# Packed products with their passes grouped by the weight's part, another order of the opening, and the memory heads' turns one product sooner

## The reference

```python
h = rms_norm(x, g_pre)                                    # 512 x 2048
proj = h @ w_in          # qa ka va ga | qb kb vb gb | fb | qm gm : widths 4*768, 4*768, 6, 2*512
out_a = moba_attention(qa, ka, va, rel_bias)              # 6 heads of 128, T5 bias
out_b = forgetting_attention(qb, kb, vb, cumsum(log_sigmoid(fb + b_forget)))   # 6 heads
km, vm = split(rms_norm(mem, g_mem) @ w_mem_kv)           # memory: 256 x 2048 -> 2 * 512
out_m = memory_attention(qm, km, vm)                      # 4 heads, 256 memory tokens
y = concat([out_a * silu(ga), out_b * silu(gb), out_m * silu(gm)])
out = x + rms_norm(y @ w_out, g_post)
```

## Time and profile before

| | us |
|---|---|
| median of 3 runs | 901.62 (901.34 to 902.13) |
| profiled execution | 902.28 |
| its span, first to last instruction | 900.5 |
| TensorE busy | 871.3 |
| VectorE busy | 733.1 |
| ScalarE busy | 537.8 |
| strips of the memory and opening, until the first packed pass | 186.8 |
| one pair of packed strips | 45.0 |

### The profile page before, as it was taken

One profiled execution on the slowest core, in us unless ns is written; L12 is line 12 of the kernel. 1 busy time (PEld: TensorE's weight loads), 2 busy tenths in 40 slices (PEclk: granted clock), 3 DMA queues, 4 the chain that ended last, 5 costly groups with the idle time before them and its releaser, 6 DMA issues.

```text
span 900.5 us, 13815 instructions
## 1 busy us (share of the span) xinstructions
PE 871.3 (97%) x5181; PEld 764.1 (85%) x5181; DVE 733.1 (81%) x1070; ACT 537.8 (60%) x932; POOL 76.6 (9%) x84
## 2 busy tenths in 40 slices
PE   8998999999999999999999999999999999999995
PEld 6888998987888888888888888888888877778884
DVE  5889978888888888888888888888988885975558
ACT  5794665555656565656565656565656585565452
POOL 0000220000000000000030303030301000000000
PEclk9999999999999999999999999999999999999998
DMA  9961567467668568667667667567653397465854
GB/s 304 284 167 48 164 165 154 118 174 164 165 142 210 151 167 185 154 175 177 152 176 175 153 175 175 152 176 175 152 129 106 130 364 272 154 220 189 290 199 186
DMA packets 179143, 161.37 MB, mean 179 GB/s; under 512 B 7353, under 2 KB 144217, under 8 KB 177670
## 3 DMA queue, kind: packets, MB, share of 16 engines
q1 hardware_dynamic: 169942, 141.62, 51.2%
q0 software_dynamic: 8704, 16.78, 13.6%
q10 hardware_dynamic: 432, 2.10, 0.7%
HBM read 152.33 MB, written 43.28 MB: 217 GB/s over the span
## 4 chain that ended last, share of the span: by engine, by line
PE 71%; DVE 15%; ACT 8%; issue 5%; POOL 1%; DVEq 0%; ACTq 0%; POOLq 0%
PE d_ps L703 18%; PE e_ps L703 10%; PE d_ps L705 9%; PE e_ps L705 5%; PE c_ps L703 4%; DVE ring L1459 3%; PE pt_ps L810 3%; ACT ring L1017 3%; PE c_ps L705 2%; PE d_ps L653 2%; PE d_ps L655 2%; PE d_ps L654 2%; DVE sums L1486 2%; PE score_ps L654 1%; PE score_ps L655 1%
## 5 line engine op out<-in xcount | busy, mean ns | idle before, releaser
L1459 DVE TENSOR_TENSOR ring<-raw,ring 128x1024 fp32r<-128x1024 f32 x134 | 164.7, 1231 | 53.1 <-ACT ring L1017 53.0
L703 PE MATMUL d_ps<-late,ring 128*128 128x512 f32 x576 | 206.6, 398 | 1.2 <-DVE five L1586 1.2
L1459 DVE TENSOR_TENSOR ring<-sums,ring 128x1024 fp32r<-128x1024 f32 x112 | 137.6, 1228 | 52.2 <-ACT ring L1017 51.9
L1017 ACT ACTIVATE ring<-raw 128x1024 fp32r<-128x1024 f32 x134 | 140.6, 1058 | 43.8 <-PE d_ps L655 17.2
L705 PE MATMUL d_ps<-late,ring 128*128 128x256 f32 x576 | 161.5, 280 | 0.0
L703 PEld LDWEIGHTS d_ps<-late,ring 128*128 128x128 f32 x576 | 108.1, 188 | 26.4 <-DVE five L1586 1.5
L1017 ACT ACTIVATE ring<-sums 128x1024 fp32r<-128x1024 f32 x112 | 118.1, 1055 | 20.0 <-DVE sums L1486 18.4
L705 PEld LDWEIGHTS d_ps<-late,ring 128*128 128x128 f32 x576 | 108.8, 189 | 0.0
L703 PE MATMUL c_ps<-tok,ring 128*128 128x512 f32 x192 | 69.3, 400 | 0.0
L703 PE MATMUL e_ps<-late,ring 128*128 128x512 f32 x192 | 69.1, 399 | 0.0
L703 PE MATMUL e_ps<-tok,ring 128*128 128x512 f32 x192 | 69.0, 399 | 0.0
(11 more groups left out here) (392 smaller groups left out, 2001.5 us busy)
## 6 DMA issues: line engine op xcount, KB each, us to landing
raw<-in_w_in_dram SPq DMA_DIRECT2D x112, 512.0 KB, 5.4
sum_dram<-in_w_out_dram POOLq DMA_DIRECT2D x32, 512.0 KB, 7.4
raw<-sum_dram SPq DMA_DIRECT2D x32, 512.0 KB, 3.9
raw<-in_w_out_dram SPq DMA_DIRECT2D x24, 512.0 KB, 7.3
raw<-in_w_mem_kv_dram SPq DMA_DIRECT2D x16, 512.0 KB, 8.6
sum_dram<-in_w_out_dram SPq DMA_DIRECT2D x16, 512.0 KB, 6.4
sum_dram<-sum_dram SPq DMA_DIRECT2D x16, 512.0 KB, 6.0
stage<-in_x_dram SPq DMA_DIRECT2D x4, 1024.0 KB, 9.7
```

The source lines that it names most:

```text
L703: pe.matmul(bank[:], w[:, 0, k], both[:, k], start=i in (TOK_A, TOK_B) and k == 0, stop=False, skip_group_check=True)
L1017: act.activation(dst, src, ACTF.Copy).then_inc(hi_done, 1)
L1459: return dve.tensor_tensor(dst, a_, hi_.bitcast(F32), ALU.subtract)
```

## The change

1. In a packed product the 8 passes with the high weight part come first, after a wait for the high part alone, then the 8 with the low part.
2. The opening: the gains are loaded on ScalarE's queue and the memory tiles on SyncE's; of 14 warm-up products 4 stay and 10 go between the two halves of the first turn; ScalarE and VectorE take memory banks and weight pieces in another order; the statistics of the memory come in t = 1 and its spread in t = 2; the squares of a token tile come one t later; the key strips are taken in t = 2, 3, 3 and 4 (`KEYS_DURING`), strips 0, 1 and 2 keeping three banks; the value strips' splits and turns and the first operands move among each other.
3. A memory head's turn comes after product D (i = 3) and its product with the values after F (i = 5), with the splits in step.

```diff
-SQUARE_DURING = {0: 2, 1: 3, 2: 4, 3: 5}
-SCALE_DURING = {1: 2, 2: 3, 3: 4, 4: 5}
+SQUARE_DURING = LOAD_DURING
+SCALE_DURING = LOAD_DURING
+KEYS_DURING = {2: (0,), 3: (1, 2), 4: (3,)}
...
-KEEP_WARM = 14
+KEEP_WARM = 4
+BETWEEN_HALVES = 10
...
+        def mem_strip(t):
+
+            bank = (d_ps + [e_ps])[t] if t < 3 else d_ps[(t - 3) % 2]
+            return bank[:, 0:NMEM]
...
-                if t >= 2:
-                    pe.wait_ge(mem_free, t - 1)
+                if t >= 3:
+                    pe.wait_ge(mem_free, t - 2 if t < 5 else t - 1)
...
-                pe.wait_ge(lo_done, operand(p, i) + 1)
...
+                if packed(p):
+                    pe.wait_ge(hi_done, operand(p, i) + 1)
+                    for k in range(KH):
+                        pe.matmul(bank[:], w[:, 0, k], both[:, k], start=i in (TOK_A, TOK_B) and k == 0, stop=False,
+                                  skip_group_check=True)
+                pe.wait_ge(lo_done, operand(p, i) + 1)
                 for k in range(KH):
                     if packed(p):
-                        pe.matmul(bank[:], w[:, 0, k], both[:, k], start=i in (TOK_A, TOK_B) and k == 0, stop=False,
-                                  skip_group_check=True)
                         last = pe.matmul(bank[:, T2:S], w[:, 1, k], hi[:, k], start=False, stop=k == KH - 1,
                                          skip_group_check=True)
...
-                if t == 1:
+                if t == 2:
                     spread_rstd()
...
             forget_gates(1, TOK_D, slice(0, T2))
-            turn_v_mem(NM - 1)
             pe.wait_ge(bank_taken, TURNS)
             forget_gates(3, TOK_F, slice(T2, S))
+            turn_v_mem(NM - 1)
...
-                    if i == 4:
+                    if i == 3:
                         turn_probs(head, 0)
                         turn_probs(head, 1)
-                    if i == 6:
+                    if i == 5:
                         prob_times_v(head)
...
+                if t in SQUARE_DURING:
+                    squares(SQUARE_DURING[t])
+                    root(SQUARE_DURING[t], SQUARE_DURING[t])
+                for m in KEYS_DURING.get(t, ()):
+                    act.wait_ge(mem_free, m + 1)
+                    act.activation(kmv[:, 2 * m], k_mem[:], ACTF.Copy).then_inc(k_hi, 1)
                 if t in TURN_DURING:
                     if t == 3:
                         act.wait_ge(gain_negated, 1)
                     take_tokens(*TURN_DURING[t])
-                if t in SQUARE_DURING:
-                    squares(SQUARE_DURING[t])
-                    root(SQUARE_DURING[t], SQUARE_DURING[t])
...
+                if keys:
+                    take_keys(keys[0])
+                if t in SCALE_DURING:
+                    scale_tile(SCALE_DURING[t])
+                if t > NM:
+                    copy_v_mem(t - 1)
+                if t != 1:
+                    lo_next(t, 1)
+                if keys:
+                    lo_keys(keys[0])
+                for m in keys[1:]:
+                    take_keys(m)
+                    lo_keys(m)
```

More of the change, by code:

```diff
@@ L504, in load_tile @@
                 sp.dma_start(stage[:, t % 4], token_tile(t)).then_inc(stage_landed[t - MB], 16)
-            for i, g in enumerate((g_mem, g_pre)):
-                sp.dma_start(gain_rows[:, i], g.rearrange("a (k p) -> (a k) p", p=P)).then_inc(gain_rows_landed, 16)
             def load_memory(half):
                 cols = slice(D // 2 * half, D // 2 * (half + 1))
-                sp.dma_start(stage[:, 1, cols], token_tile(1)[:, cols]).then_inc(mem_landed[1][half], 16)
+                for i in range(MB):
+                    sp.dma_start(stage[:, i, cols], token_tile(i)[:, cols]).then_inc(mem_landed[i][half], 16)
             def load(m, src):
@@ L670, in strip @@
                             pe.wait_ge(bank_taken, kt // 2 + 1)
-                        last = three(d_ps[t % 2][:, 0:NMEM], (w[:, 0, k], w[:, 1, k]), (mem_tile(0, kt), mem_tile(1, kt)),
+                        last = three(mem_strip(t), (w[:, 0, k], w[:, 1, k]), (mem_tile(0, kt), mem_tile(1, kt)),
                                      kt == 0, kt == KT - 1)
@@ L836, in _ @@
             turn_tiles(0, 0)
+            for i in range(BETWEEN_HALVES):
+                pe.matmul(v_mem_ps[i % 2][:], waste[:, 0:P], waste[:, 0:S], start=True, stop=True)
             turn_tiles(0, 1)
@@ L1220, in hi_pt @@
                 last.then_inc(pt_hi, 1)
-            for half in range(2):
-                cols = slice(D // 2 * half, D // 2 * (half + 1))
-                act.dma_start(stage[:, 0, cols], token_tile(0)[:, cols]).then_inc(mem_landed[0][half], 16)
+            for i, g in enumerate((g_mem, g_pre)):
+                act.dma_start(gain_rows[:, i], g.rearrange("a (k p) -> (a k) p", p=P)).then_inc(gain_rows_landed, 16)
             act.wait_ge(pool_consts, 2)
@@ L1238, in hi_next @@
                         hi_operand(0, half)
-                if t != 1:
-                    hi_next(0)
+                hi_next(0)
+                if t == 1:
+                    for half in range(2):
+                        act.wait_ge(mem_landed[0][half], 16)
+                    squares(0)
+                if t == STRIPS_MEM - 1:
+                    hi_v_mem(1)
+                    hi_v_mem(2)
+                    hi_late(TOK_B)
                 hi_next(1)
-                if 1 <= t <= NM:
-                    act.wait_ge(mem_free, t)
-                    act.activation(kmv[:, 2 * (t - 1)], k_mem[:], ACTF.Copy).then_inc(k_hi, 1)
                 if t == NM + 1:
@@ L1732, in _ @@
                                           ).then_inc(diag_ready, 1)
+                if t == 2:
+                    dve.wait_ge(rstd_spread, 1)
+                    chain(dve.tensor_copy(rstd_mem[:], c_ps[:, 0:NMEM]))
+                if keys:
[11 more added lines that the diff above has]
+                    lo_keys(m)
+                if t == 6:
+                    lo_v_mem(0)
                 if t in TURN_DURING:
```

91 lines of the change are left out of this document (37 added, 54 removed).

## The result

| | before | changed |
|---|---|---|
| median, us | 901.48 (901.28 to 902.13, 4 runs) | 914.22 (913.07 to 916.74, 4 runs) |
| ratio | | 1.0137, 95% interval 1.0125 to 1.015 |
| span of the profiled execution | 900.5 | 914.9 |

Slower, as forecast, but by 12.7 us where 3.6 was the sum, and outside the range of 897 to 911.5. The profiled execution is the longest of the four (916.74), so the trace shows 14.4 us of difference and the median 12.7.

What follows compares the result with a forecast made beforehand. TensorE's pace was taken to bound the packed stretch, VectorE and ScalarE the opening. Terms -6.3 + 3.8 + 4.4 + 1.7 = +3.6 us on 902.3, less 0.7 for the median, gave 905.2 us; range 897 to 911.5.

Steps and rivals of the forecast that it cites:

- Packed term: 24 packed strips: ordering passes by weight part saves 6 ns for each of 1344 pairs, less two losses: -6.3 us.
- The smaller deduction: 12 gate and value strips: faster products become waiting at the turn of the first probabilities, 2 x 0.05 us each, 1.3 us.
- the bound of 0: Packed products: the upper bound of their term, no gain if the pace of the passes stays.
- Rival 4: Packed products: the passes' order gives nothing, as spacing follows from columns only; 911.5 us, chance 0.08.
- Opening: Opening: ScalarE waits for the third key strip, token banks start 5.1 us later, product C of strip 0 late: +3.8 us.
- My bounds: Opening: -1.4 us if product C starts once its low part is there at 92.0, +5.5 if the clock falls too.
- neither TensorE nor its clock decides there: Opening: removing two TensorE stalls and their half-clock stretches gains nothing, because VectorE decides and ScalarE sets VectorE's start.
- Heads: Memory heads: turn and values come sooner but probabilities do not, so TensorE waits and the next strips start late: +4.4 us.
- +1.7 for the clock: Memory strip 2: the longest stall, some 4.5 us, is followed by 3.4 us at half clock, charged once: +1.7 us.
- Rival 3: Memory heads and product C: the clock falls at further stalls, three at 1.7 us each; 910.3 us, chance 0.15.
- Rivals 1 and 2: Memory heads' turn costs nothing, 899.1 us, chance 0.25; the opening isn't held, 900.0 us, chance 0.12.

Runs made afterwards that it cites:

- the filled kernel: Kernel before with only the memory heads' turn and values one product sooner, plus 7, 18, 10 and 9 idle matmuls ahead of the turns: 907.81 us, ratio 1.0062.
- groups of eight: Kernel before with only the packed product's passes ordered by the weight's part, eight long then eight short: 900.08 us, ratio 0.9973.
- joined rows: Packed order by the weight's part, with products C, E and G taking their short passes first so that long passes join: 899.98 us, ratio 0.9975 to before.

## Why the prediction was wrong, point by point

**Packed term: -6.3 predicted, -2.4 measured (order alone), -2.0 in the changed kernel's trace.** Right sign, mis-sized. The step that failed is "a 512-column pass takes 389 ns where only 512-column passes follow each other", carried from the output stage, where rows are long, to rows of eight. There a long pass comes to its steady 227 ns only with the sixth: from start to start eight long passes average 230 ns, 4 less than in turn, not 9, and even the steady pace is only 7 less. The short passes came about as forecast, 2 ns dearer (3). That leaves 1.75 ns for each of 1344 pairs, 2.4 us. I had put 0.5 us in all on the first long passes of a group, "until the stream is even"; they cost 4 to 5 us (3 to 3.6 ns for each of 1344 passes), the largest part of the error. (The smaller deduction, 2 x 0.05 us in 12 strips, is 1.2 and not 1.3 us.) With no row for a group of eight, the value had to lie further towards the bound of 0. Rival 4, that the order gives nothing, is excluded by 0.9973 (0.9963 to 0.9984). A spacing that follows from the columns, as the Trainium skill gives it (page "TensorE: Matmul & The Clock Gate", section "Back-to-back issue gap"), is the same for every pass of a width; the trace has 233 ns at the start of a row of 512-column passes and 227 at its end.

**Opening: +3.8 predicted, +6.0 measured.** The chain was right at each place that it named: token banks 47.08 (46.5), the next ones 57.33 (56.8), product C 97.03 (96.3), behind a stall of 3.6 us (3.6), with A 0.6 us later and not at the same time. What was missing is the clock behind that stall: C runs at about 0.50 and takes 4.4 us (5.2 with the opening alone) instead of 2.9. Of the +6.0, 3.9 are C's late start and 2.3 the clock in the trace of the opening alone. My bounds had it as the far end; the rows that I had myself cited for such stalls said it would be so. The step "neither TensorE nor its clock decides there" also failed: moving the last value turn alone makes C 1.9 us later, and holding the clock up there makes it 0.8 us sooner.

**Heads: +4.4 and +1.7 for the clock predicted, +9.7 measured.** The mechanism was right: probabilities not sooner, stalls of 1.7, 4.5, 2.5 and 2.3 us ahead of the turn ("2 to 4.5"), E pushed behind them. With the clock held up the three strips cost 2.3, 1.8 and 1.0 us (2.4, 0.6 and 1.2 predicted), 5.1 against 4.2. The step that failed is the clock: I gave it one of the four stalls. In the changed kernel it fell behind all four; in the heads alone behind three, worth some 4 us. The waits were nearly right, with an offsetting pair of slips. The forecast 10.5 us from the end of normalising to the next strip is what the filled kernel has (10.6 in each of the three). But I took the slack from the low part of the next strip's third weight, and the next strip begins right behind product G, so the 10.5 had to be set against 8.3, 9.3 and 9.3 us before: +2.2, +1.2 and +1.2. And in strip 2 the normalising itself starts 0.6 us later after product A, in strip 3 0.2 us sooner. That gives the 2.3, 1.8 and 1.0.

**Clock.** Rival 3, "the clock falls at every head and before product C", was worked out at 910.3 us with a chance of 0.15, and it is what happened. The trace of the changed kernel can be added up. For the clock I take what C needs more than its 2.9 us, then how much longer than in the filled kernel the way from normalising to the next strip is (12.1, 12.6 and 11.8 us against 10.6), and for the fourth head the length of the strip (27.2 against 26.0); these are estimates.

| term | predicted, us | in the trace, us |
|---|---|---|
| waits: product C late (3.7), the four heads (2.3, 1.8, 1.0, 0.2) | +8.2 | +9.0 |
| clock: product C (1.5), the four heads (1.5, 2.0, 1.3, 1.2) | +1.7 | +7.5 |
| passes' order | -6.3 | -2.0 |
| sum | +3.6 | +14.5 (14.4 measured) |

So two errors stood on top of each other, the size of the packed term and the rank of that rival; the waits were mis-sized by less than 1 us. Between the medians the difference is 1.7 us smaller, and so is its clock term: filling the stalls gave back 3.6 us, about 5 if the overrun of 1.1 us is added. Rival 3 holds 6.8 us of clock. That 910.3 with the packed term at -2.4 in place of -6.3 comes to 914.2 us, the median to the last digit, is therefore luck; the mechanism isn't. Rivals 1 and 2 are out: the heads' turn costs 9.7 us, and the opening was held.

**What would show it.** Right: token banks, product C, the stalls. Wrong: long passes at 395 ns on average (389), the packed pair at 44.8 us (44.4), the first packed pass at 201.8 (195). "Slower" came true because opening and heads each cost time alone, as forecast.

## What to carry to other kernels

A stall that an edit adds on TensorE should be charged twice, with its length and with the half-clock stretch behind it: here that stretch followed most of the added stalls of 1.7 us and more, though not all, and cost 1.2 to 2.3 us each. If a stall can't go, idle matmuls in it give that back, so long as they don't run over. A step is moved sooner only together with the chain that feeds it: the turn ahead of its probabilities cost 9.7 us, the same turn with the reciprocal moved too 3.1. And a duration taken from a long uniform stretch isn't that of a short row.

## What was unexpected of the hardware

- A row of equal passes has a beginning: behind passes of the other width and weight, 512-column passes start 233 and 236 ns apart, then 228 to 233, and settle at 227 with the sixth; in turn with short ones they stay at 234.
- The length of a stall alone doesn't tell whether the clock falls. With the turn in place and the reciprocal sooner, TensorE stood 2.66 us at 150 us and went on at 1.00; with the heads moved and the reciprocal sooner it stood 2.69 us at the same time and went on at 0.50; in the changed kernel 1.7 us was enough in strip 1. Even the same stall in the same code goes both ways. The stall ahead of the last value turn, in the kernels with groups of eight and with joined rows (timeline of TensorE, then the busy time behind it, in this order):

```profile
83.66 0.44 PE L743 MATMUL e_ps<-ident,vT 128*128 128x128 f32 x2 [3.18 <-DVE vT L1637]
...
83.78 0.44 PE L759 MATMUL e_ps<-ident,vT 128*128 128x128 f32 x2 [3.17 <-DVE vT L1653]
```

```profile
85.00:88.40 3.40, 3.40 (x18) 3.12 (x16) 3.40 (x4) 1.32 (x1) 0.00 (x0) 0.50 0.00 0
...
85.00:88.40 3.40, 3.16 (x26) 2.82 (x24) 3.40 (x4) 1.45 (x1) 0.00 (x0) 1.00 0.00 0
```

  These two kernels differ only in the packed products, which come 100 us later. What decides is open.
- The time of the changed kernel spreads by 3.7 us over four runs, that of before by 0.9 over four and by 2.4 over the twenty of one comparison. The mean granted clock of the changed kernel's runs lies between 0.982 and 0.988, with the lowest at the longest.
